# Twelve gate tiles as pairs of seven block products ahead of the retention, and the final projection summed over all of K in PSUM

## The reference, cut to what is computed

```python
z = h @ w_in                       # columns: rq rk rv rg fq fk fv ff gr gf
y_ret = silu(rg) * group_norm(retention(rotary(rq), rotary(rk), rv))   # 4 heads
y_fox = forgetting_attention(fq, fk, fv, log_sigmoid(ff + b_f))        # 8 heads
merged = sigmoid(gr) * (y_ret @ ret_proj) + sigmoid(gf) * (y_fox @ fox_proj)
x = x + g1 * (merged @ w_out)
h2 = modulate(rms_norm(x))
x = x + g2 * ((silu(h2 @ w_gate) * (h2 @ w_up)) @ w_down)    # width 2816
return rms_norm(x)
```

## Time and profile before

| | us |
|---|---|
| runs | 1919.75, 1920.45, 1921.56; median 1920.45 |
| the profiled execution: its span from first to last instruction | 1921.5 |
| its own time: the slowest of the three runs agrees with the span | 1921.56 |
| TensorE busy | 1858.8, 97% of the span, 8706 matmuls |
| TensorE weight loads | 1543.0, 80% |
| VectorE, ScalarE, GpSimd busy | 1096.8 (57%), 639.2 (33%), 962.1 (50%) |

### The profile page before, as it was taken

The page is one execution under the profiler, slowest core; times in us unless marked ns, Lnnn a source line. Parts: engine busy times, 40 slices in busy tenths (PEclk is TensorE's granted clock), DMA queues, the critical chain, the costliest instruction groups (busy, mean ns, idle before and its releaser), DMA issues.

```text
span 1921.5 us, 24108 instructions
## 1 busy us (share of the span) xinstructions
PE 1858.8 (97%) x8706; PEld 1543.0 (80%) x8706; DVE 1096.8 (57%) x1644; ACT 639.2 (33%) x1155; POOL 962.1 (50%) x589
## 2 busy tenths in 40 slices
PE   4989999999999999999999999989999999999998
PEld 3878888888878878888888888777888888878887
DVE  6875454554666766565564444384555655556637
ACT  5541323223333223322231001274444444442123
POOL 1233435262677775436317646829878888800000
PEclk8998999999999999999999999999999999999999
DMA  9451112021544425122105122222444444399864
GB/s 387 175 197 35 45 27 62 24 55 25 191 151 156 171 99 169 59 89 71 44 23 197 44 66 77 70 95 85 146 144 163 155 142 154 132 374 370 300 221 174
DMA packets 177265, 257.49 MB, mean 134 GB/s; under 512 B 9209, under 2 KB 121753, under 8 KB 174881
## 3 DMA queue, kind: packets, MB, share of 16 engines
q1 hardware_dynamic: 167458, 222.75, 34.5%
q10 hardware_dynamic: 9728, 33.67, 4.8%
HBM read 186.89 MB, written 69.51 MB: 133 GB/s over the span
## 4 chain that ended last, share of the span: by engine, by line
PE 84%; DVE 4%; ACT 2%; issue 2%; POOL 2%; DMA 2%; ACTq 0%; DVEq 0%; POOLq 0%
PE ps L931 52%; PE ps L1385 10%; PE ps L1386 10%; PE ps L1387 10%; PE ps L1281 1%; DMA b_da<-f_units 1%; POOL b_wu L893 1%; DVE b_macc L2063 1%; DVE b_probs L2383 0%; ACT b_act_q L1889 0%; PE ps L1149 0%; DMA b_macc<-in_ada_w 0%; PE ps L1217 0%; PE ps L1091 0%; POOL b_wsum L888 0%
## 5 line engine op out<-in xcount | busy, mean ns | idle before, releaser
L931 PE MATMUL ps<-b_hT,b_w_split 128*128 128x512 f32 x3104 | 761.7, 396 | 0.8 <-DVE b_macc L2063 0.8
L931 PEld LDWEIGHTS ps<-b_hT,b_w_split 128*128 128x128 f32 x3104 | 572.1, 189 | 112.9 <-DVE b_macc L2063 1.2
L765 POOL TENSOR_TENSOR b_spare<-b_w_stage 1x1 f32<-1x1 f32 x80 | 19.8, 248 | 493.0 <-PE ps L931 453.2
L1385 PE MATMUL ps<-b_act_q,b_wu 128*128 128x512 f32 x616 | 241.0, 391 | 8.8 <-DVE b_act_q L2063 4.6
L1386 PE MATMUL ps<-b_act_q,b_wu 128*128 128x512 f32 x616 | 240.5, 390 | 0.0
L1387 PE MATMUL ps<-b_act_q,b_wu 128*128 128x512 f32 x616 | 240.3, 390 | 0.0
L766 POOL TENSOR_SCALAR b_w_split<-b_w_stage 128x1024 fp32r<-128x1024 f32 x80 | 221.0, 2763 | 0.2
L768 POOL TENSOR_TENSOR b_w_split<-b_w_stage,b_w_split 128x1024 fp32r<-128x1024 f32 x80 | 195.6, 2445 | 6.7
L893 POOL TENSOR_TENSOR b_wu<-b_raw,b_wu 128x512 fp32r<-128x512 f32 x110 | 165.5, 1514 | 57.7 <-ACT b_wu L1832 57.5
L1385 PEld LDWEIGHTS ps<-b_act_q,b_wu 128*128 128x128 f32 x616 | 116.0, 188 | 35.4 <-issue 10.6
L2063 DVE TENSOR_TENSOR b_cb<-ps,b_snap 128x512 f32<-128x512 f32 x66 | 45.3, 687 | 167.5 <-PE ps L1387 166.8
(11 more groups left out here) (241 smaller groups left out, 2933.6 us busy)
## 6 DMA issues: line engine op xcount, KB each, us to landing
f_units<-b_fu SPq DMA_DIRECT2D x70, 512.0 KB, 2.6
b_w_stage<-in_w_in SPq DMA_DIRECT2D x65, 512.0 KB, 4.0
down_units_d<-b_wd SPq DMA_DIRECT2D x66, 256.0 KB, 2.0
b_da<-f_units SPq DMA_DIRECT2D x11, 1536.0 KB, 6.4
b_dr<-down_units_d SPq DMA_DIRECT2D x14, 1024.0 KB, 10.1
b_da<-f_units SPq DMA_DIRECT2D x7, 2048.0 KB, 8.0
b_wd<-in_w_down SPq DMA_DIRECT2D x11, 1024.0 KB, 5.1
b_raw<-in_w_gate SPq DMA_DIRECT2D x22, 512.0 KB, 4.5
```

Of the source, the lines that this page charges most:

```text
L765: pool.tensor_tensor(spare[0:1, :], src[0:1, 0:1], src[0:1, 0:1], ALU.add)
L931: return pe.matmul(o, l, r, start=start, stop=stop)
L1385: pe.matmul(o, l[0], r[0], start=begin and at == 0, stop=False, skip_group_check=go_on)
```

## The change

The table of tiles starts with two gate tiles (`T_GATE`), and retention's tiles come behind (`T_RET = 2`).

- **Gate stage.** `first_jobs` now makes the two gate tiles of block 0. Behind the opening come six pairs (GR and GF of block k = 1 to 6), each as seven *units*: a unit is a product of a 512 x 128 block of weights (or a sum of such) with a 512 x 512 block of hT (or a difference of such), 12 matmuls. `A_SEQ` gives the order: pairs 0 and 1 interleaved, the others one after another. A unit's weights are made into a ring of eight places `a_wu`, which lies over the four slots of w_split. SP loads a pair's weights into `a_raw` (1 MB, two places); GpSimd makes four sums per pair (`a_total`) and the low parts (`a_low`), ScalarE the high parts (`a_hi`), a copy of the banks (`a_snap`) and the sigmoids (`a_gate`), VectorE the combinations (`combine`) and the differences of hT (`hc`). The gates go to DRAM (`gates_d`). The later ada_w pieces are 32 of 512 KB: 16 in this stage, 16 in head 0, the sums 1024 wide.
- **Retention.** Head 0 is like the others; GpSimd makes all its tiles. Its first tile follows the last unit.
- **Last head.** It has the two gate tiles of block 7 between its steps, 96 matmuls.
- **Projection.** w_out's eight row blocks are scaled, split and all kept; the merge of each block and half of the frames is one of sixteen (`MERGES`, the first on GpSimd); ScalarE's queue brings gates and ret_merge per merge (`mix_load`). TensorE sums over all eight k in PSUM: first the eight banks of frames 0 to 511 (per k 24 matmuls), then four banks (12 per k), then four banks one by one. VectorE adds each bank to resid once (`add_out`). The last w_out roundings are ScalarE's (`wo_high`).

```diff
-T_RET = 0
+T_GATE = 0
+T_RET = T_GATE + 2
-T_WO = T_FOX + FOX_TILES * (FH - 1) + 2
+T_WO = T_FOX + FOX_TILES * FH
+A_PAIRS = KT - 2
+A_RING = 8
+A_SEQ = [(0, 0), (0, 3), (1, 0), (1, 3), (0, 1), (1, 1), (0, 2), (1, 2), (0, 5), (1, 5), (0, 4), (1, 4), (0, 6), (1, 6)]
+A_SEQ += [(p, u) for p in range(2, A_PAIRS) for u in range(Q7)]
+A_TURN = 4
+LATER = 4 * KT
...
+        def a_slot(i):
+            return (i + A_TURN) % A_RING
...
+        K_SEQ = (0, 7, 1, 2, 3, 4, 5, 6)
+        MERGES = ((7, 0), (1, 0), (0, 1), (2, 0), (7, 1), (3, 0), (4, 0), (5, 0), (6, 0),
+                  (1, 1), (2, 1), (3, 1), (4, 1), (5, 1), (6, 1))
...
+            def a_raw_load(p):
+                if p >= 2:
+                    sp.wait_ge(ua_rdy, a_made(p - 2))
...
+            sp.wait_ge(a_s, TT * FH)
+            for half in range(2):
+                sp.dma_start(g0[:, half, :, :], gates_d[0, half]).then_inc(m_g0, 16)
+            sp.wait_ge(a_tr, 2 * FH)
+            sp.dma_start(mret[:, 0, :], ret_merge[:, 0:S]).then_inc(m_ret[0], 16)
+            for i in range(3):
+                wo_load(i)
+            sp.wait_ge(a_pv, 12 * FH)
+            sp.dma_start(mret[:, 1, :], ret_merge[:, (KT - 1) * S:KT * S]).then_inc(m_ret[1], 16)
+            for i in range(3, 6):
+                wo_load(i)
+            sp.wait_ge(m_sum, MERGE_AT[KT - 1, 1] + 1)
+            sp.dma_start(resid[:, :, :], x_v).then_inc(s_xagain, 16)
+            for i in range(6, KT):
+                wo_load(i)
...
             for j in range(RET_TILES):
-                low_tile(j)
+                if j < SLOTS:
+                    slot = slot_turn(T_RET, j)[0]
+                    pool.wait_ge(ua_used, 1 + max(i for i in range(A_UNITS) if a_slot(i) // 2 == slot))
+                tile(T_RET, j)
...
-                    fill = [16, 26] + [28 + 2 * n for n in range(len(steps) - 1)]
+                fill = [16, 32] + [36 + 6 * n for n in range(len(steps) - 1)]
...
+            for m in range(len(MERGES)):
+                act.wait_ge(m_sum, m + 1)
+                if m in after:
+                    mix_load(after[m])
+                merged_hi(m)
+                if m in (0, 2, 3, 5):
+                    wo_high({0: 4, 2: 5, 3: 6, 5: 7}[m])
```

1215 lines of the change are left out of this document (741 added, 474 removed).

## The result

| | before | after |
|---|---|---|
| median of the runs, us | 1920.1 (1919.72 to 1921.56) | 1956.53 (1955.49 to 1959.47) |
| ratio, 95% interval | | 1.0191 [1.0176, 1.0205] |
| span of the profiled execution | 1921.5 | 1953.7 |
| TensorE busy, matmuls | 1858.8, 8706 | 1854.9, 8634 |
| mean granted clock, of 1 | 0.991 | 0.981 |

The change makes the kernel 1.9% slower: 36.4 us. That is the predicted side with three times the predicted size (+12.2, 1933.7), and beyond the range, which ended at 1941.

A forecast was written before the change was run, and what follows sets the result against it. TensorE was taken as the bound nearly everywhere. Against the profiled 1921.5 us, -16.3 - 8.5 + 7.7 + 7.3 - 1.0 + 23.5 - 0.5 = +12.2 gave 1933.7; own range 1927 to 1939, with the rivals 1908 to 1941.

The forecast's parts named there:

- step 3: Gate stage, start of the third pair: TensorE idles 5.8 to 6 us plus 1.7 of clock; +7.7 (4.5 to 9).
- step 2: Retention's head 0: smaller ada loads and half-wide sums recover all but 1 of 9.5 us lost; -8.5 (-4 to -9.5).
- step 6: Last projection: 25.5 us of waits beyond 87.2 of matmuls, less 2.0 idle before; +23.5.
- step 7: Behind the projection: first FFN weights made during its second half, one add per bank instead of two; -0.5.
- Step 4: End of the gate stage: retention's tile 0 waits for the last units' slot, 5.5 us plus 1.7 of clock; +7.3 (5.5 to 8).
- Step 5: Last head: 96 instead of 48 filling matmuls fill waits, a sigmoid table load costs 0.5; -1.0 (0 to -1.5).
- (a): Projection's start: late w_out rows and the first merge leave TensorE 7.0 us idle after T', the last head's own product's end.
- (b): Projection's fifth K step: w_out's seventh block, queued behind the residual, lands at T' + 35.4; 14.8 to 15.1 us idle.
- (c): Projection's rest: four more steps, 21.8 us, then a second half of 192 matmuls, 43.6, ending at T' + 112.7.
- The seventh block doesn't queue behind the residual: Rival, projection: w_out's block lands 3.7 to 7.7 us after issue; 9.9 less, 1923.8, no change; chance 0.16.
- The projection keeps pace: Rival: the merges finish before TensorE asks, with no more waits than the 2.0 us of before; 1910; chance 0.27.
- More of the same: Rival: slower GpSimd in the gate stage (+2), residual at 19.4 (+6), merges at their slow rate (+3); 1945; chance 0.13.

The follow-up runs named there:

- e4: Changed kernel with head 0's last three ada sums placed between VectorE's first four bank copies instead of ahead of them: 1950.54 us, ratio 1.0161.
- e2: Changed kernel with ScalarE's copy of pair 0's last bank moved ahead of the roundings for the third pair's units: 1948.41 us, ratio 1.0133.
- c1: Changed kernel with VectorE's sixteen differences and low parts of hT in the gate stage made plain one-input copies (wrong values): 1950.23 us, ratio 1.0161.
- e3: Changed kernel with the ring of units turned so the last two units lie in the slot of retention's tile 1: 1949.16 us, ratio 1.0142.
- e6: Changed kernel with the last norm's row (512 KB) loaded later in the down product: 1952.05 us, ratio 1.016.
- e1: Changed kernel with the residual's 4 MB load moved on SP behind the last of w_out's eight blocks: 1946.83 us, ratio 1.0128.

## Why the prediction was right in its direction and wrong in its size

The direction was right for the reasons given: all four long waits came where they were forecast, and together they outweigh the 16.3 saved. The size failed. Of the 20.0 missing between +12.2 and +32.2, step 3 has 6.2, step 2 has 5.9, step 6 has 3.9, step 7 has 3.0, steps 4 and 5 have 1.9, and the opening gave 0.9 back.

- **Step 1** (-16.3) is exact: 8706 - 8634 = 72 matmuls.
- **Step 2** (head 0, -8.5 taken, -4 the poorer end) failed: -2.6. "I leave 1 of the 9.5" was the failing sentence. From head 0's rotation to head 1's it takes 361.41 - 238.12 = 123.3, against 103.6 + 12.6 without loss. The sums are half as wide, but the last three were still ahead of the bank copies in VectorE's list, and e4, which moves them, gives 6.2 back. The order of VectorE's list would have told this; I had priced the sums by their width and not by what stands behind them.
- **Step 3** (+7.7, up to 9) was right in place, chain and releaser, which e2 confirms, and too small: +13.9. The step that failed is GpSimd "at 1.29, the shortest of their kind", where VectorE works beside it. Three things make the 6.2. GpSimd's operations from 66 to 95 us were taken at 1.29 and took 2.2; this gave two waits of 1.4, 2.8, that weren't in the sum, and moved the load by 5.4, which the wait shows as 2. The restart clock was 3.1 in all, not 1.7. c1 takes most of the collision away: the load lands on the predicted time and the stage is 6.0 shorter.
- **Step 4** (+7.3) was right: 5.5 of wait to the tenth, 8.4 with a clock of 0.50 behind. e3 removes the wait whole, and two of 1.24 and 1.31 come in the tiles behind.
- **Step 5** (-1.0): -0.2, inside its range.
- **Step 6** (+23.5, measured +27.4): (a) the start at T' + 7.25 for 7.0; (b) the landing at T' + 39.1, inside 33.7 to 41, but 3.7 later than taken, and the fifth step at T' + 47.7 for 45.6. (c) was right in content. Missing were 1.2 of short waits and 2.3 of clock. That the long wait measured 15.45 for 14.8 to 15.1 is in part luck. From the residual's issue to the block's landing it took 13.9 for the 14.1 taken, which was right. But the issue came 3.9 late, what stands behind the landing took 8.6 for 10.2 (the loads are issued without waiting for the rounding's end), and TensorE came 1.8 late itself. VectorE at "0.69, since such operations are short where GpSimd waits" was the choice that failed: four operations took 2.3 to 2.9, two of them ahead of the residual's issue, two in the 0.80 at the sixth step. The mean of 1.18 in the earlier trace rows hid this already: eight of the fourteen operations took 0.69, the other six 1.21 to 2.88.
- **Step 7** (-0.5, measured +2.5) missed that the last norm's row, a load of 0.5 MB, now stands in SP's list among the down product's first loads; before, it stood among those of the first gate and up products, and the text of the change doesn't say that it moved. e6 shows the wait shrink from 3.0 to 1.2, and the product by 3.4.
- **The rivals.** "The seventh block doesn't queue behind the residual" is refuted by 13.5 us from issue to landing; in e1, ahead of the residual, the same block landed in 3.6. (The wait that it gives is 35.7 - 30.5 = 5.2 and not 4.9; its 9.9 less is right.) "The projection keeps pace" is refuted by the two long waits. "More of the same" came nearest, since it had GpSimd's rate and the merges' slow rate, and at 1945 was still 8.7 short of the profiled span of 1953.7: it left out head 0, the norm's row and the clock, and its largest term, the residual at 19.4 (+6), didn't come.
- **The range** ended at 1941 because it had ends for the waits that the prediction saw and none for what it didn't: the sums ahead of the copies, the norm's row and part of the clock. GpSimd's and VectorE's rates, one cause, moved steps 3 and 6 the same way. The reference adds 4.2 (36.4 against 32.2): 3 for the place of before's profiled execution, which was taken as 1.1 above the median, and 1.0 for the changed kernel's.

By what its removal alone gave in its stretch, the places weigh: e1's chain 7.1, the slot 6.9, the projection's start 6.4, head 0's sums 6.2, the third pair 5.2, the norm's row 3.4; all removed together, 28.2.

What stays open: which of the edits ahead of the forgetting heads lose 5 of the 7 us when they are put together, and how far the gate stage could be freed. GpSimd's operations in the opening were not split, and no run gave its gate sums to another engine.

## What to carry to other kernels

A product scheme that saves TensorE under 1% of its matmuls pays only if the engines that feed it have slack in the very stretch, and not on average: GpSimd at 50% of the span was full where it counted, and an operation of it can hold up VectorE. Price a moved stage with operations at their rate beside the other engine's, look at the spread behind a mean, and keep up to 3 us of clock for each stall of TensorE on top of its length. When a large load joins a queue, look for the small one behind it; a load that isn't needed for 15 us belongs behind those that are, and in pieces.
